# Compressed queries and index keys in the first two of eight projection slots, their chain and the top-k between the other slots

## What is computed

```python
def hybrid_ab_mixer(u, table, w_in, cq_g, wq_b, wq_idx, w_out):
    proj = u @ w_in                                  # 1024 -> 2856 columns
    qa, ka, va, cq, kb, vb, k_idx, w_idx = jnp.split(proj, ...)   # 512 512 512 256 512 512 32 8
    o_a = dilated_mixture(qa, ka, va, table[:, :8])  # 8 heads of 64
    cq = rmsnorm(cq, cq_g)                           # compressed queries, 256 wide
    qb = cq @ wq_b                                   # 8 heads of 64
    q_idx = cq @ wq_idx                              # 8 index heads of 32
    o_b = dsa_attention(qb, kb, vb, q_idx, k_idx, w_idx, table[:, 8:], topk=64)
    return concatenate([o_a, o_b]) @ w_out

# in dsa_attention, for each block of 128 queries:
#   sc = relu(q_idx . k_idx); score = sum_h w_idx[h] * sc[h], causal
#   each query keeps the 64 keys of highest score and attends to those alone
```

## Time and profile before

| | us |
|---|---|
| time before, median of 3 (lowest to highest) | 1673.91 (1673.51 to 1674.88) |
| the profiled execution's own time | 1673.79 |
| its span | 1671.8 |
| busy: PE, PEld, DVE, ACT, POOL | 1554.4, 1352.5, 1140.2, 814.1, 42.5 |

### The profile page before, as it was taken

How to read it: one execution, slowest core, us unless ns; L and a number is a source line. 1 busy time by engine, 2 the same in 40 slices (tenths; PEclk the granted TensorE clock), 3 DMA queues, 4 the chain that set the end, 5 groups by cost and what they waited for, 6 DMA issues and landing times.

```text
span 1671.8 us, 26989 instructions
## 1 busy us (share of the span) xinstructions
PE 1554.4 (93%) x9148; PEld 1352.5 (81%) x9148; DVE 1140.2 (68%) x1740; ACT 814.1 (49%) x1308; POOL 42.5 (3%) x53
## 2 busy tenths in 40 slices
PE   7898786999999989999996999999999999999997
PEld 6788674898898958888894788888788878888886
DVE  5845863798788947777544657777777765667775
ACT  6423442777677744444443453444444445654442
POOL 1120000000000000000000100000000000000000
PEclk9898787999999999999997599999999999999999
DMA  6312231799799947555451056556456544155552
GB/s 255 114 64 76 76 107 38 252 353 348 262 338 348 351 172 229 188 188 189 139 182 57 1 172 200 193 187 193 152 187 193 189 155 152 54 173 189 188 188 76
DMA packets 82148, 299.67 MB, mean 179 GB/s; under 512 B 9278, under 2 KB 9406, under 8 KB 81952
## 3 DMA queue, kind: packets, MB, share of 16 engines
q1 hardware_dynamic: 79632, 289.97, 51.6%
q0 software_dynamic: 2160, 8.66, 1.7%
q10 hardware_dynamic: 288, 0.12, 0.0%
HBM read 297.59 MB, written 1.11 MB: 179 GB/s over the span
## 4 chain that ended last, share of the span: by engine, by line
PE 85%; DVE 9%; ACT 4%; issue 1%; DMA 0%; POOL 0%; DVEq 0%; SPq 0%; POOLq 0%; ACTq 0%
PE ps L1680 17%; PE ps L1505 15%; PE ps L1506 14%; PE ps L1507 14%; PE ps L1678 10%; PE ps L1511 3%; PE ps L1677 2%; PE ps L1632 2%; DVE w_lo L921 2%; PE ps L1604 1%; PE ps L1697 1%; DVE xT L960 1%; PE ps L1772 1%; ACT arena L600 1%; ACT w_hi L545 1%
## 5 line engine op out<-in xcount | busy, mean ns | idle before, releaser
L921 DVE TENSOR_TENSOR w_lo<-raw,w_hi 128x1024 fp32r<-128x1024 f32 x549 | 653.4, 1221 | 230.7 <-ACT w_hi L545 229.5
L545 ACT ACTIVATE w_hi<-raw 128x1024 fp32r<-128x1024 f32 x549 | 549.1, 1055 | 337.6 <-PE ps L1507 306.4
L1680 PE MATMUL ps<-xT,w_hi 128*128 128x512 f32 x1232 | 439.6, 396 | 0.0
L1678 PE MATMUL ps<-xT,w_lo 128*128 128x256 f32 x1408 | 364.5, 279 | 0.0
L1678 PEld LDWEIGHTS ps<-xT,w_lo 128*128 128x128 f32 x1408 | 265.3, 188 | 16.1
L1680 PEld LDWEIGHTS ps<-xT,w_hi 128*128 128x128 f32 x1232 | 231.2, 188 | 47.1
L1505 PE MATMUL ps<-w_hi,xT 128*128 128x256 f32 (+2 forms) x848 | 261.6, 309 | 7.0 <-DVE w_lo L921 3.6
L1506 PE MATMUL ps<-w_lo,xT 128*128 128x256 f32 (+2 forms) x848 | 251.9, 297 | 0.0
L1507 PE MATMUL ps<-w_hi,xT 128*128 128x256 f32 (+2 forms) x848 | 251.8, 297 | 0.0
L1505 PE MATMUL ps<-w_hi,h_hi 128*128 128x512 f32 x480 | 188.4, 392 | 4.4 <-DVE h_lo L1121 4.4
L1506 PE MATMUL ps<-w_lo,h_hi 128*128 128x512 f32 x480 | 187.7, 391 | 0.0
(11 more groups left out here) (315 smaller groups left out, 1630.0 us busy)
## 6 DMA issues: line engine op xcount, KB each, us to landing
raw<-in_wstream SPq DMA_DIRECT2D x549, 512.0 KB, 5.0
arena<-bias_rows POOLq DMA_DIRECT2D x2, 2048.0 KB, 12.2
const<-in_const POOLq DMA_DIRECT2D x1, 1112.0 KB, 7.5
x_res<-in_x SPq DMA_DIRECT2D x2, 512.0 KB, 4.5
arena<-in_mem POOLq DMA_DIRECT2D x1, 1024.0 KB, 5.3
out<-arena SPq DMA_DIRECT2D x2, 512.0 KB, 2.7
smallw<-in_smallw POOLq DMA_DIRECT2D x1, 768.0 KB, 4.4
prow<-in_prow POOLq DMA_DIRECT2D x1, 512.0 KB, 5.1
```

What stands on the lines that cost most here:

```text
L545: nc.scalar.activation(w_hi[:, slot, lo:hi], raw[:, slot, lo:hi], ACT.Copy).then_inc(S_(f"hi_{part_}"), 1)
L921: tt(w_lo[:, slot, lo:hi], raw[:, slot, lo:hi], w_hi[:, slot, lo:hi].bitcast(F32), ALU.subtract).then_inc(S_(f"lo_{part_}"), 1)
L1678: low = mm(bank[:, 0:S], w_lo[:, s, c:c + P], xT_hi[:, k, :], start=False, stop=False)
L1680: last = mm(bank, w_hi[:, s, c:c + P], both, start=False, stop=k == KD - 1)
```

## The change

The tile list of the hybrid projection is reordered: slot 0 holds `cq` (two tiles) and the index weights, slot 1 the index keys and two tiles of `qa`, slots 2 to 7 the rest, in the order `qa`, `ka`, `kb`, `va`, `vb`. The weights are packed on the host in the same order. The chain's steps and the top-k then stand between the slots:

```diff
-        flat = [("T", v[:, j, :]) for v in (h_qaT, h_kaT, h_kbT) for j in range(4)] + [("T", kiT)]
-        flat += [("N", cq, 0), ("N", cq, 128)] + [("N", v, 128 * j) for v in (h_va, h_vb) for j in range(4)]
-        flat += [("W", widx, 0)]
+        flat = [("N", cq, 0), ("N", cq, 128), ("W", widx, 0), ("T", kiT)]
+        flat += [("T", v[:, j, :]) for v in (h_qaT, h_kaT, h_kbT) for j in range(4)]
+        flat += [("N", v, 128 * j) for v in (h_va, h_vb) for j in range(4)]
...
@@ ScalarE @@
-            for n in range(HYB0, HOUT0):
-                proj(n)
+            proj(HYB0)
+            split_all(HYB0 + 2)
             act.wait_ge(S_("cq_ss"), 1)
             nc.scalar.activation(hss[:, 0:2], hss[:, 0:2], ACT.Sqrt, ...
+            evacuate_slot(HYB0 + 1)
             act.wait_ge(S_("cq_tr"), 1)
...
+            proj(HYB0 + 2)
+            split_all(HYB0 + 4)
             act.wait_ge(S_("qb_psum"), 1)
...
+            evacuate_slot(HYB0 + 3)
             for t in range(T):
+                split_all(HYB0 + 5 + t)
                 act.wait_ge(S_("idx_psum"), t + 1)
                 if t:
                     act.wait_ge(S_("idx_sum"), t)
                 nc.scalar.activation(relu..., ACT.Relu).then_inc(S_("relu_ready"), 1)
+                evacuate_slot(HYB0 + 4 + t)
+            for n in range(HYB0 + 6, HOUT0):
+                proj(n)
             attention(*ATT2)
@@ VectorE @@
-            for n in range(HYB0, HOUT0):
-                proj(n)
-
-            dve.wait_ge(S_("evacuated"), evac_until(HOUT0 - 1))
+            split_all(HYB0 + 1)
+            dve.wait_ge(S_("evacuated"), evac_until(HYB0))
             link(tt(cqsq, cq, cq, ALU.mult))
             nc.vector.tensor_reduce(hss[:, 0:2], cqsq, AX.X, ALU.add).then_inc(S_("cq_ss"), 1)
+            split_all(HYB0 + 2)
             dve.wait_ge(S_("head_std"), 3)
...
             link(ts(widx, widx, 2.0 ** -4, None, ALU.mult))
+            split_all(HYB0 + 3)
+            split_all(HYB0 + 4)
             for t in range(T):
+                split_all(HYB0 + 5 + t)
...
                 link(tt(s_, s_, cst("causal")[:, S * t:S * t + w], ALU.add))
+                if t:
+                    split_all(HYB0 + 7)
+                for r in range(TOP_ROUNDS):
+                    top_round(t, r)
+            split_all(HOUT0)
             dve.wait_ge(S_("bias_loaded"), 16)
-            attention(*ATT2, rounds=[(t, r) for t in range(T) for r in range(TOP_ROUNDS)])
+            attention(*ATT2)
@@ TensorE @@
-            for n in range(HYB0, HOUT0):
-                proj(n, 5 if n == HYB0 else None)
-            pe.wait_ge(S_("evacuated"), evac_until(HOUT0 - 1))
+            proj(HYB0, 5)
+            proj(HYB0 + 1)
             pe.wait_ge(S_("cq_scaled"), 1)
...
             ins.then_inc(S_("cq_tr"), 1)
+            proj(HYB0 + 2)
             pe.wait_ge(S_("cqT_ready"), 1)
...
             ins.then_inc(S_("qb_psum"), 1)
+            proj(HYB0 + 3)
             pe.wait_ge(S_("qb_ready"), 1)
             for t in range(T):
                 if t:
+                    proj(HYB0 + 4)
                     pe.wait_ge(S_("relu_ready"), t)
...
                 ins.then_inc(S_("idx_psum"), 1)
+            for n in range(HYB0 + 5, HOUT0):
+                proj(n)
+            pe.wait_ge(S_("evacuated"), evac_until(HOUT0 - 1))
             pe.wait_ge(S_("relu_ready"), T)
             attention(*ATT2)
```

More of the change, by code:

```diff
@@ L549, in proj, with evacuate_slot @@
                 if n + 1 < N_SLOTS and n >= OUT0:
[L550 to L553, removed]
+                    split_all(n + 1)
+                if evacuate:
+                    evacuate_slot(n)
+            def evacuate_slot(n):
                 act.wait_ge(S_("d_used"), n + 1)
@@ L863, in _ @@
                 S_("head_std"), 1)
+            evacuate_slot(HYB0 + 1)
             act.wait_ge(S_("cq_tr"), 1)
             for k in range(2):
-                ins = nc.scalar.activation(cqT[:, k, :], ps[:, 4, S * k:S * k + S], ACT.Copy, scale=pc("cq_g")[:, k:k + 1])
+                ins = nc.scalar.activation(cqT[:, k, :], ps[:, 3, S * k:S * k + S], ACT.Copy, scale=pc("cq_g")[:, k:k + 1])
             ins.then_inc(S_("cqT_ready"), 1)
+            proj(HYB0 + 2)
+            split_all(HYB0 + 4)
             act.wait_ge(S_("qb_psum"), 1)
-            nc.scalar.activation(h_qbT.rearrange("p j s -> p (j s)"), ps[:, 5:7, :].rearrange("p b s -> p (b s)"), ACT.Copy)
-            nc.scalar.activation(qiT.rearrange("p j s -> p (j s)"), ps[:, 7, :], ACT.Copy).then_inc(S_("qb_ready"), 1)
+            nc.scalar.activation(h_qbT.rearrange("p j s -> p (j s)"), ps[:, 0:2, :].rearrange("p b s -> p (b s)"), ACT.Copy)
+            nc.scalar.activation(qiT.rearrange("p j s -> p (j s)"), ps[:, 2, :], ACT.Copy).then_inc(S_("qb_ready"), 1)
+            evacuate_slot(HYB0 + 3)
             for t in range(T):
+                split_all(HYB0 + 5 + t)
                 act.wait_ge(S_("idx_psum"), t + 1)
@@ L1027, in out_quad, with attention @@
                 ins.then_inc(S_("att_out"), 1)
-            def attention(u0, u1, rounds=()):
+            def attention(u0, u1):
                 for i in range(u0, u1 + 4):
@@ L1035, in attention @@
                         combine_unit(i - 1)
[L1036 to L1039, removed]
                     if u0 <= i - 4 < u1 and (i - 4) % QUAD == QUAD - 1:
@@ L1966, in _ @@
                 for t in range(T):
-                    ins = flip(ps[:, 4, S * k + P * t:S * k + P * t + P], cq[:, t, P * k:P * k + P])
+                    ins = flip(ps[:, 3, S * k + P * t:S * k + P * t + P], cq[:, t, P * k:P * k + P])
             ins.then_inc(S_("cq_tr"), 1)
+            proj(HYB0 + 2)
             pe.wait_ge(S_("cqT_ready"), 1)
@@ L1973, in _ @@
                 for k in range(2):
-                    ins = mm(ps[:, 5 + j // 2, S * (j % 2):S * (j % 2) + S], wq[:, k, P * j:P * j + P], cqT[:, k, :],
+                    ins = mm(ps[:, j // 2, S * (j % 2):S * (j % 2) + S], wq[:, k, P * j:P * j + P], cqT[:, k, :],
                              start=k == 0, stop=k == 1)
             ins.then_inc(S_("qb_psum"), 1)
+            proj(HYB0 + 3)
             pe.wait_ge(S_("qb_ready"), 1)
@@ L2108 @@
     _projection_slots(ws, HYB0, _tiles(_np.concatenate(
-        [qa, ka, kb, ki, ki, ki, ki, cq, va, vb, wi, _np.zeros((D, P - 8), f32)], 1), 24))
+        [cq, wi, _np.zeros((D, P - 8), f32), ki, ki, ki, ki, qa, ka, kb, va, vb], 1), 24))
     _projection_slots(ws, HOUT0, _tiles(a["hyb_w_out_2"][0], 8))
```

## The result

| | before | after |
|---|---|---|
| time, median of 20 runs each (lowest to highest) | 1674.9 us (1673.09 to 1676.05) | 1658.4 us (1651.51 to 1679.73) |
| the profiled execution's own time, its span | 1673.79, 1671.8 | 1659.05, 1657.0 |

The ratio is 0.990, 95% interval 0.9893 to 0.9907: 1.0% faster, some 16.5 us, where 27.7 were forecast.

The account below looks back on a forecast made before the run. TensorE bounds the slots; behind them lie a chain with idle engines and an attention at 1.2 GHz. Scores at 895.9 + 33.7 + 6.4 put `norm(6)` at 936.0, 27.7 less: 1673.8 - 27.7 = 1646 us, range 1638 to 1656.5.

Parts of the forecast that it names:

- Slots and chain: Eight slots with the chain's matmuls between them: 68.4 + 7.65 us at full clock, ending at 894.5, scores at 895.9.
- rival 3: Slots starve as ScalarE and VectorE wait for each other: slower, 1677 us or more; chance 0.02.
- rival 4: Some chain step finds its input late and the chain stays exposed: 1672 to 1676 us; chance 0.01.
- VectorE's lateness: At the hybrid attention's entrance: first maximum 1.4 us after the first scores instead of 0.6, so 0.8 late.
- The clock at the entrance: Hybrid attention's entrance: TensorE does 0.93 of 3.7 us, so the clock falls there more often than not.
- The clock before `ATT3`: Between the two hybrid attention calls: the clock rises in the first's last units, so the second runs at full clock.
- The term for the clock: First hybrid attention call at low clock: four pairs add 10.6 us, less 3.4 and 0.8 covered idle time, + 6.4.
- rival 2: Clock falls and stays low to the last units: + 14, `norm(6)` at 943.4, 1653.5 us, upper bound 1656.2; chance 0.31.
- The attention at the held clock: Both hybrid attention calls at full clock, first scores to `norm(6)`: 30.45 + 0.8 + 2.4 = 33.7 us.
- What the low clock costs: Both hybrid attention calls: eight pairs add 21.3 us, less ramps, lateness and some 2 for a late rise: + 14.
- The upper end of the range: 1656.5 us, from today's hybrid attention unshortened but for 3 us of waiting for index sums.

Follow-up runs that it names:

- run 2: Changed kernel with VectorE's split of the first output slot moved from ahead of the first maximum into the hybrid attention; 1654.0 us, ratio 0.9896.
- run 6: Changed kernel with GpSimd's first masks held back until VectorE has done the second maximum; 1653.9 us, ratio 0.9879.
- run 1: Changed kernel with filler matmuls (5 and 9) in the two TensorE gaps at the hybrid attention's entrance; 1651.7 us, ratio 0.9861.
- Run 8: Changed kernel with late split, one attention call of 16 units, and fillers at the hybrid and last attention's entrances; 1638.2 us, ratio 0.9785.
- run 7: Changed kernel with top-k rounds back beside the first attention's units and the entrance filled (5 and 5 matmuls); 1679.1 us, ratio 1.0031.
- run 10: Run 8's kernel with the top-k rounds back beside the first eight units and the split ahead of the attention; 1660.3 us, ratio 0.9915.
- run 3: Changed kernel with the top-k rounds back beside the first attention's units, only the chain staying moved; 1675.2 us, ratio 0.9995.
- 9b: Run 8's kernel without its fillers at the last attention's entrance; 1642.6, 1653.2, 1639.0 and 1655.0 us, ratio 0.985.

## Why the prediction was wrong

In the profiled execution the miss is 1659.05 - 1646 = 13.1 us. Its parts, by the prediction's steps, with the 2.1 us by which this execution was already late at `norm(5)` (818.05 for 815.92) taken off:

- **Slots and chain, right.** Last slot's end and scores were forecast at 894.5 and 895.9; 898.36 - 2.13 = 896.2. By the spacing of starts the twelve matmuls took 5.0 (846.72 to 851.71) for 5.2 forecast and the four transposes 0.35 (837.66 to 838.01) for 0.45, no slot waited, and nothing of the chain or the top-k stands on the path. Rivals 3 and 4 are out. One thing was not foreseen and does no harm: ScalarE twice waits for `raw` in the slots, since VectorE frees it later.

```profile
884.56 1.06 ACT L545 ACTIVATE w_hi<-raw 128x1024 fp32r<-128x1024 f32 x1 [1.08 <-DMA raw<-in_wstream]
...
892.44 1.06 ACT L545 ACTIVATE w_hi<-raw 128x1024 fp32r<-128x1024 f32 x1 [0.57 <-DMA raw<-in_wstream]
```

- **VectorE's lateness, mis-sized:** the first maximum comes 2.37 behind the first scores, where 1.4 was forecast and 0.6 would be punctual; so 1.8 late for 0.8. I had said of the masks that they "were made during the attention and still are" and had set the key mask's 3 us earlier at nothing. The masks moved to beside the split, and each slowed the other: 3.50 to 5.09 and 1.95 to 3.78 (runs 2 and 6).
- **The clock at the entrance, right:** it fell at 900.2, within 4 us of the last slot, and run 1 shows that the gaps did it.
- **The clock before `ATT3`, the step that failed:** "`ATT2` now ends with the same sequence and no rounds beside it, so I expect the clock back before `ATT3`". It came back at 951.4, after `norm(6)` had begun. The term for the clock was + 6.4 and should have been rival 2's. Two things stand behind that. A rise in the drain, which runs 2 and 6 show, is undone by the second entrance a few microseconds later; a sequence that had ended a stage in the trace before was carried to a place with another ramp behind it. And in the profile of after it did not even rise there. What differs in runs 2 and 6 is an entrance 2 us shorter and a fall at another moment; which of the two decides is open, and was not tried apart.
- **The attention at the held clock, right:** 33.7 was forecast from the first scores to `norm(6)`, and run 1, whose maximum comes as late as after, took 34.5.
- **What the low clock costs, mis-sized:** rival 2 had + 14 for both calls, and the terms named there give still less (21.3 - 2 x 3.4 - 0.8 - 2 = 11.7): with a slip of my own in it, 943.4 for `norm(6)`. Measured is 946.2, its stated upper bound of 946.1; between runs with the clock low and held lie 130.3 - 114.8 = 15.5. I had taken off 2 for a rise near the end that did not come.
- Together 946.2 - 936.0 = 10.2; 2.1 before the stage; 0.6 behind it (`norm(6)` to `norm(7)` 31.38 us for 30.76). That is 12.9 of 13.1.

The upper end of the range was rival 2's bound for this stage alone. It held nothing for what an execution gains or loses in stages that the change doesn't touch, and 2 us of that were enough to leave it.

The Trainium skill, "TensorE: Matmul & The Clock Gate", section "Why this matters for your kernels", warns of long idle gaps between bursts, and these gaps, none of them long, would pass by it. The measurement decides: gaps of 1.22 and 2.37 us with 0.93 us of matmuls between them took the clock for 51 us, and in run 2 one of 1.21 and one of 0.61 did. The remedy that follows from it, work in the gap, is right: run 1.

What was gained in the stage, by the profiled executions: 16.5 us of the 17.5 by the chain's place, 1 by the top-k's. Run 8 shows 36.8 to be there (147.8 to 111.0). The other 19.3 hang on the clock, and the top-k's place, worth 1 us as built, is what makes them attainable (runs 7 and 10).

## What to carry to other kernels

When dense work is followed by a stage that ramps up through two or three engines, look at each entrance of the stage, and at each place where it drains and refills, for the share of time that TensorE is busy; fill those gaps with matmuls that nobody reads, since a lost clock made an attention of 30.45 us one of 48.1. A change that only moves side work off the path can read as worth 1 us in its stage while the clock is low, and be worth 20 once it is held: test it in both. And where the time of one kernel spreads, as in run 3, compare the stages of a profile beside the medians, since the two can say different things. Last, before work of one elementwise engine is moved, see what the other one will be doing at its new place.

## What the runs showed of the hardware

- **The same program keeps or loses the clock from one execution to the next.** The last mixer's attention took 30.45 us in the profiles of before and after and 48.1 in those of runs 1 and 7, with the same code; run 3's ten executions spread over 20 us, 9b's four over 16, while the 20 of before lay within 3 (three other sets of before, 46 executions in all, spread over 3.6 to 7.3, none with a mean clock under 0.951). That the last attention, untouched, would lose 17.6 us in some executions of the kernels changed in an earlier stage was not foreseen. What decides it in an execution can't be read from these traces.
- **Once low, the clock can stay low under work that looks dense.** From 903.60 to 948.35 TensorE was busy 43.26 of 44.75 us at 0.50. In the drains of runs 2 and 6 it rose, in the same sequence of after it did not.
- **VectorE and GpSimd slow each other** when a split and two masks run side by side: 3.49 to 5.09 us and 1.95 to 3.78. Parted, each takes its old time: 3.49 for the split in run 6, 1.96 for the masks in run 2. Both began within 0.23 us of each other, and the later end is 5.09 after the start, near the 5.44 of one behind the other. The Trainium skill, "SBUF — State Buffer", section "SBUF: two separate sides", has the rule: a VectorE operation with two SBUF inputs and a GpSimd operation that reads SBUF exclude each other for a whole instruction. The trace agrees; had the masks' new place been looked up against it, the lateness could have been forecast.
